# Recurrent branch: one left operand for two products, and its transpose beside them in crossed tiles

## The reference, cut to what matters

```python
def step(S, inp):
    r_t, w_t, k_t, v_t, a_t, b_t = inp
    sa = jnp.einsum('bhij,bhj->bhi', S, a_t)
    S = S * w_t[:, :, None, :] + sa[..., None] * b_t[:, :, None, :] + v_t[..., None] * k_t[:, :, None, :]
    y = jnp.einsum('bhij,bhj->bhi', S, r_t) if emit else None
    return S, y
```

## Time and profile before

| | us |
|---|---|
| median of 3 runs | 2735.48 (2731.41 to 2739.09) |
| profiled execution, its own time | 2739.95 |
| its span in the trace | 2738.2 |
| TensorE busy | 2606.0 |
| VectorE busy | 1708.3 |
| ScalarE busy | 928.2 |
| GpSimd busy | 831.3 |

### The profile page before, as it was taken

How to read it: one execution, slowest core, us unless ns; L and a number is a source line. 1 busy time by engine, 2 the same in 40 slices (tenths; PEclk the granted TensorE clock), 3 DMA queues, 4 the chain that set the end, 5 groups by cost and what they waited for, 6 DMA issues and landing times. The chain is left out here.

```text
span 2738.2 us, 60351 instructions
## 1 busy us (share of the span) xinstructions
PE 2606.0 (95%) x25068; PEld 2077.8 (76%) x25068; DVE 1708.3 (62%) x3073; ACT 928.2 (34%) x2146; POOL 831.3 (30%) x1067
## 2 busy tenths in 40 slices
PE   7989999999999999999999999999999899999998
PEld 4978798795654887868688867777888677858886
DVE  5657767764525846764753358659833676577675
ACT  2013323223422225642221148321211576122571
POOL 3323344240013520012322215235531344246010
PEclk9999999999999999999999999999999999999999
DMA  6321100102432013303011152131111311122100
GB/s 235 106 95 57 45 13 9 39 15 96 156 107 91 32 62 140 125 1 108 33 62 62 62 191 68 53 115 58 36 62 62 139 63 62 62 84 93 79 3 31
DMA packets 108464, 206.05 MB, mean 75 GB/s; under 512 B 21955, under 2 KB 26194, under 8 KB 107680
## 3 DMA queue, kind: packets, MB, share of 16 engines
q1 hardware_dynamic: 107920, 201.30, 21.0%
q0 software_dynamic: 272, 0.89, 0.1%
HBM read 186.85 MB, written 15.54 MB: 74 GB/s over the span
## 5 line engine op out<-in xcount | busy, mean ns | idle before, releaser
L739 PE MATMUL psum<-weights,h_t 128*128 128x256 f32 x1488 | 355.2, 382 | 5.5 <-ACT early_work L828 5.5
L739 PEld LDWEIGHTS psum<-weights,h_t 128*128 128x128 f32 x1488 | 280.8, 191 | 45.3 <-ACT early_work L828 6.7
L739 PE MATMUL psum<-z_l,x_tiles 128*128 128x256 f32 x816 | 192.8, 379 | 0.5 <-POOL z_l L954 0.5
L1528 DVE TENSOR_REDUCE neg_max<-psum 128x1 f32<-128x768 f32 x160 | 147.1, 955 | 69.0 <-PE psum L1304 58.7
L739 PEld LDWEIGHTS psum<-z_l,x_tiles 128*128 128x128 f32 x816 | 155.0, 190 | 21.9 <-issue 0.9
L839 ACT ACTIVATE early_work<-psum 128x512 f32<-128x512 f32 (+1 forms) x80 | 45.0, 565 | 364.7 <-DVE psum L1112 248.1
L1477 ACT ACTIVATE prob<-psum,neg_max 128x768 f32<-128x768 f32 x128 | 114.1, 897 | 80.4 <-DVE neg_max L1528 80.4
L1112 DVE TENSOR_TENSOR psum<-psum,early_work 128x512 f32<-128x512 f32 x62 | 43.1, 696 | 146.3 <-PE psum L739 146.3
L1600 POOL TENSOR_TENSOR z_l<-z_l,inv_total 128x128 f32<-128x128 f32 x64 | 25.3, 400 | 310.4 <-DVE inv_total L1536 310.4
L739 PE MATMUL psum<-weights,x_tiles 128*128 128x256 f32 x496 | 117.2, 379 | 0.0
L790 PE MATMUL psum<-weights,h_t 128*128 128x512 f32 x256 | 111.5, 593 | 1.2 <-PEq L240 1.2
(11 more groups left out here) (545 smaller groups left out, 6661.2 us busy)
## 6 DMA issues: line engine op xcount, KB each, us to landing
weights<-in_ada_w_dram SPq DMA_DIRECT2D x30, 2048.0 KB, 8.2
weights<-in_a_w_in_dram SPq DMA_DIRECT2D x10, 2048.0 KB, 8.0
weights<-in_b_w_in_dram SPq DMA_DIRECT2D x8, 2048.0 KB, 8.6
weights<-in_c_w_in_dram SPq DMA_DIRECT2D x8, 2048.0 KB, 8.8
weights<-in_w_in_dram SPq DMA_DIRECT2D x6, 2048.0 KB, 8.7
x_aside<-x_tiles SPq DMA_DIRECT2D x24, 512.0 KB, 2.6
x_tiles<-x_aside SPq DMA_DIRECT2D x4, 3072.0 KB, 15.9
weights<-in_a_w_out_dram SPq DMA_DIRECT2D x4, 2048.0 KB, 7.9
```

What stands on the lines that cost most here:

```text
L739: last = pe.matmul(dst, lhs[:, k, :], rhs[k // 2][:, k % 2, :], start=k == 0, stop=k == KH - 1)
L1528: dve.tensor_reduce(neg_max[:, i % 4, m:m + 1], score_at(i, m), AX, ALU.max, negate=True)\
```

## The change: what it does

1. **Groups for jobs.** The 20 jobs become six groups: b with the context of both directions, b with the sequence of direction 0, of direction 1, and the same three of k. In a sequence group each chunk and head is one matmul whose left operand is b (or k) and whose streamed side is 128 columns, 64 of a and 64 of r, in two runs of the buffer. In a context group 64 columns of a are streamed.
2. **Crossed tiles.** After the two products of a chunk come its two transposes: that of the head on partitions 0 to 63 is written to PSUM partitions 64 to 127, and the other way round, in banks of their own. ScalarE takes them back across in two copies of 64 partitions each.
3. **Who takes what.** The `nt` product is no longer masked by VectorE. VectorE reads it from PSUM with the mask of level 1 alone, ScalarE copies it out unmasked, and the level masks that follow pick the entries they need. GpSimd adds the identity. VectorE's transposed copies wait for GpSimd.
4. **Banks and waits.** A group's banks are taken again three groups later, after VectorE and ScalarE have read them; the inverse uses banks 0 to 3 in place of 4 to 7. GpSimd's masks of L4043 wait for the first three groups only.

```diff
-            for i, job in enumerate(jobs):
-                name, d, chunks, left, right, _, _ = job
-                if i >= 8:
-                    pe.wait_ge(*done(i - 8))
-                for n, c in enumerate(chunks):
-                    cols = slice(col_of(c), col_of(c) + CH)
-                    for h in range(2):
-                        s = slice(64 * h, 64 * h + 64)
-                        rhs = pr.eye[s, s] if right is None else right[s, d, cols]
-                        last = pe.matmul(pr.bank(i % 8)[s, CH * n:CH * n + CH], left[s, d, cols], rhs,
-                                         start=True, stop=True)
+            def decayed_and_read(s, d, c):
+                at = d * US + col_of(c)
+                step = 2 * US + d * SEQ - d * US
+                return flat_x[s, at:at + 2 * step].rearrange("p (two x) -> p two x", two=2)[:, :, 0:CH]
+            def multiply(g):
...
+                if g >= 3:
+                    for semaphore in seen(g - 3):
+                        pe.wait_ge(*semaphore)
...
+                        for s in halves:
+                            if seg:
+                                last = pe.matmul(pair_ps(g, 0)[s, d, n, :], left[s, d, columns(c)], b["a_f"][s, d, columns(c)],
+                                                 start=True, stop=True)
+                            else:
+                                to = pr.bank(first_bank_of(g), 2)[s, 2 * CH * n:2 * CH * n + 2 * CH]
+                                last = pe.matmul(to.rearrange("p (two t) -> p two t", two=2), left[s, d, columns(c)],
+                                                 decayed_and_read(s, d, c), start=True, stop=True)
+                        for h, s in enumerate(halves):
+                            o = halves[1 - h]
+                            to = turned_ps(g)[o, d, n, :] if seg else turned_ps(g)[o, n, :]
+                            beside = pe.matmul(to, left[s, d, columns(c)], pr.eye[s, s], start=True, stop=True)
                 last.then_inc(*multiplied.tick())
+                beside.then_inc(*turned.tick())
...
@@ block.vector
+            for d in range(2):
+                begin(1, d)
+            for d in range(2):
+                begin(0, d)
+                take("rb", d)
+            mirror_begun(0)
+            mirror_begun(1)
+            take_context()
+            mirror_begun(2)
+            mirror_begun(3)
+            for d in range(2):
+                take("ak", d)
+                take("rk", d)
...
@@ block.scalar
+            def take_n(g):
+                _, seg, d = groups[g]
+                act.wait_ge(*multiplied.at(g + 1))
+                act.wait_ge(*taken_v.at(v_order.index(("nt", seg, 1 if seg else d)) + 1))
...
+            def take_turned(g):
...
+                act.wait_ge(*turned.at(g + 1))
+                for h, s in enumerate(halves):
+                    last = act.activation(out[s], turned_ps(g)[halves[1 - h]], ACT.Copy)
+                last.then_inc(*taken_a.tick())
+            for g in range(3):
+                take_n(g)
+                take_turned(g)
+            for g in range(3, 6):
+                take_turned(g)
...
@@ block.gpsimd
+            for i, (d, seg) in enumerate(batches):
...
+                pool.wait_ge(*taken_v.at(v_order.index(("nt", seg, d)) + 1))
+                pool.tensor_tensor(t, t, wide(single(eye, 1 - d), 1, e - a), ALU.add).then_inc(*added_eye.tick())
+                pool.wait_ge(*taken_a.at(a_order.index(("nt", seg, None if seg else d)) + 1))
...
+                pool.tensor_tensor(b["levels"][0][:, d, a:e, :], b["m_ab_t"][:, d, a:e, :],
+                                   wide(masks[:, MASKS.index(name), :], 1, e - a), ALU.mult).then_inc(*levelled.tick())
```

More of the change, by code:

```diff
@@ L3722, in rwkv_core_stage, with seen, first_bank_of @@
     s_decayed = pr.counter("sc_s_decayed")
[L3723 to L3735, removed]
-    eye = masks[:, MASKS.index("eye"), :]
[L3738 to L3744, removed]
+    groups = [("b", 1, None), ("b", 0, 0), ("b", 0, 1), ("k", 1, None), ("k", 0, 0), ("k", 0, 1)]
+    v_order = [("nt", 1, 0), ("nt", 1, 1), ("nt", 0, 0), ("rb", 0, 0), ("nt", 0, 1), ("rb", 0, 1),
+               ("ak", 1, None), ("ak", 0, 0), ("rk", 0, 0), ("ak", 0, 1), ("rk", 0, 1)]
+    a_order = [("nt", 1, None), ("bt", 1, None), ("nt", 0, 0), ("bt", 0, 0), ("nt", 0, 1), ("bt", 0, 1),
+               ("kt", 1, None), ("kt", 0, 0), ("kt", 0, 1)]
+    eye = masks[:, MASKS.index("eye"), :]
+    flat_x = pr.X[:, :, :].rearrange("p t n -> p (t n)")
+    def seen(g):
+        name, seg, d = groups[g]
+        v = [i for i, x in enumerate(v_order) if x[1] == seg and (d is None or x[2] == d)
+             and x[0] in (("nt", "rb") if name == "b" else ("ak", "rk"))]
+        a = [i for i, x in enumerate(a_order) if x[1] == seg and x[2] == d and x[0] in (("nt", "bt") if name == "b" else ("kt",))]
+        return taken_v.at(max(v) + 1), taken_a.at(max(a) + 1)
+    def first_bank_of(g):
+        return (0, 2, 5, 0, 2, 5)[g]
     def single(x, odd):
@@ L3799, in _ @@
                 last.then_inc(*multiplied.tick())
+                beside.then_inc(*turned.tick())
+            for g in range(len(groups)):
+                multiply(g)
             def products(bank, lhs, rhs, i, half=None):
@@ L3835, in _ @@
                     pe.wait_ge(*x_out.at(i - 1))
-                else:
-                    pe.wait_ge(*done(14 + i))
+                elif i == 0:
+                    for semaphore in seen(3):
+                        pe.wait_ge(*semaphore)
                 products(X + i % 2, n_m[li % 2], b["inv"], i).then_inc(*x_done.tick())
@@ L3933, in _ @@
         def _(dve):
[L3934 to L3952, removed]
-                    dve.transpose(b["inv"][:, d, a:e, :], b["inv_t"][:, d, a:e, :]).then_inc(*begun_mirrored.tick())
@@ new lines, in begin @@
+            def begin(seg, d):
+                a, e = segment(seg)
+                g = 0 if seg else 1 + d
+                src = pair_ps(g, 0)[:, d] if seg else pair_ps(g, 0)
+                cols = dict(two=2)
+                src = src.rearrange("p c (s two) -> p c s two", **cols)[:, :, :, 1 - d]
+                t = b["inv_t"][:, d, a:e, :].rearrange("p c (s two) -> p c s two", **cols)[:, :, :, 1 - d]
+                first = masks[:, MASKS.index(("up1", "low1")[d]), :]
+                dve.wait_ge(*multiplied.at(g + 1))
+                ins = dve.tensor_tensor(t, src, wide(single(first, 1 - d), 1, e - a), ALU.mult)
+                ins.then_inc(*taken_v.tick())
@@ new lines, in mirror_begun, with take @@
+            def mirror_begun(i):
+                d, seg = batches[i]
+                a, e = segment(seg)
+                dve.wait_ge(*added_eye.at(i + 1))
+                dve.wait_ge(*identity.at(d + 1))
+                dve.transpose(b["inv"][:, d, a:e, :], b["inv_t"][:, d, a:e, :]).then_inc(*begun_mirrored.tick())
+            def take(name, d):
+                g = (1 if name == "rb" else 4) + d
+                mask = masks[:, MASKS.index(("up", "low")[d] + ("" if name == "ak" else "_i")), :]
+                dve.wait_ge(*multiplied.at(g + 1))
+                if name == "rb":
+                    dve.wait_ge(*taken_a.at(a_order.index(("nt", 0, d)) + 1))
+                dve.tensor_tensor(b["m_" + name][:, d, 0:XC, :], pair_ps(g, 0 if name == "ak" else 1), wide(mask, 1, XC),
+                                  ALU.mult).then_inc(*taken_v.tick())
```

63 lines of the change are left out of this document (41 added, 22 removed).

## The result

The changed kernel took 2713.9 us (median of 4 runs, 2712.51 to 2718.3) and the kernel before 2733.44 (2730.1 to 2739.09): ratio 0.9933 [0.9919, 0.9947], 19.5 us less. The forecast was 2714.

A forecast was written before the change was run, and what follows sets the result against it. TensorE's record pace was taken as the bound: products 8.9 us for 14.95, `finish(0)` at 11.4 for 16.76, 5.35 less per pair. Over four pairs that is 21.4 us off the median 2735.48, so 2714 us, range 2708 to 2731.

The forecast's parts named there:

- TensorE's pace, four tiles together: Pair products: a chunk's four tiles run together, 0.22 us per sequence chunk, 0.117 per context chunk, 8.9 us for 14.95.
- rival 2: Pair products: only two of four tiles run together, 14.4 us of products, 2730 to 2735 us in all; chance 0.13.
- Rival 1: Pair products: weight loads go in turn on shared partitions, 11.2 us of products, 2721 us in all; chance 0.15.
- Rival 3: Pair products: a tile waits for its neighbour on the same partitions, 25.6 us of products, 2778 us; chance 0.08.
- The sum: Per pair: 8.9 us of products, 9 to 9.5 from first product to inverse, `finish(0)` at 11.4 for 16.76.
- I leave that pair like the rest: Second pair before the change: its products take some 0.9 us more than the first's; treated like the other pairs.
- the wrong-sized term: ScalarE's 15 copies, 0.60 us each, 0.5 start to start, from 1.8 us; `finish(0)` may start at 10.9 or 11.0.
- The forecast of 11.4: `finish(0)` starts 11.4 us after a pair's first product, for 16.76 before: 5.35 us less per pair.
- GpSimd and VectorE's waits: GpSimd's fourth identity addition ends at 9.0 to 9.9 us; VectorE's read that `finish(0)` needs ends at 10.7 to 11.6.
- rival 4: Products shrink, but waits on ScalarE's copy or GpSimd's additions eat the gain; 2725 us with half of it; chance 0.06.
- Worth nothing by itself: VectorE: dropping its two identity instructions (1.38 us each on a sequence block) and the unmasked part of `nt` gains nothing.
- The inverse and the scan follow: Behind the products: inverse and scan keep their instructions and move up whole; the inverse still takes 28.9 us.

The follow-up runs named there:

- e1_diag: Changed kernel with the transposes put back on the diagonal tiles, on their own rows, products still joined: 2732.42 us, ratio 0.9991 to the kernel before.
- e3_same_rows: Changed kernel with a chunk's four matmuls issued head by head, product then transpose: 2721.75 us, ratio 0.9944 to the kernel before.
- e6_repeat: Changed kernel with each pair's first group multiplied nine times over, 512 records more per pair: 2775.99 us, ratio 1.0143 to the kernel before.
- e4_split: Changed kernel, still crossed, with each 128-column product split into two of 64, 512 records per pair: 2730.6 us, ratio 0.9984 to the kernel before.
- e7_no_k_turned: Changed kernel without the transposes of k, 96 records fewer per pair, so another output: 2713.67 us, ratio 0.9925 to the kernel before.
- e8_vector_eye_early: Changed kernel with VectorE adding the identity right behind begin's read, ahead of GpSimd's masks: 2718.37 us, ratio 0.9945 to the kernel before.
- e2_vector_eye: Changed kernel with VectorE, not GpSimd, adding the identity just ahead of each transposed copy: 2739.69 us, ratio 1.0018 to the kernel before.
- e5_early_step: Changed kernel with the inverse's first product issued ahead of the last group: 2718.7 us, ratio 0.9937 to the kernel before.
- run 80: Not a run's label: TensorE "had run 80 records", that is, executed them, in the unaltered changed kernel's rerun (2714.97 us, ratio 0.9925 to the kernel before).

## Why the prediction was right

- **TensorE's pace, four tiles together: held.** A sequence chunk costs 0.22 us, as worked out. Crossing gives this pace (e1_diag without it: 14.47 us), and rival 2, which had just that number, fell. Rival 1, loads in turn, would be 11.2 us; the pairs have 9.4 to 10.5. In the rerun two pairs took 11.6 and 11.8, but of these one has 2.0 us of holes and the other a lower clock.
- **Rival 3 fell** in the changed kernel and again in e3_same_rows, where it would have been 25.6 us of products for 9.31. The rule of the Trainium skill behind it ("TensorE: Matmul & The Clock Gate", "The mechanism": a weight load overlaps a matmul only when its row group is another) does not hold here: the trace has 0.22 us a chunk, where it would have 0.566; two tiles on the same partitions run together in either order.
- **What the pace leaves out: the supply of instructions.** The sum had 8.9 us for the products and "9 to 9.5" to the inverse; two pairs took 10.5. The second had two holes, 10.53 − 9.51 = 1.02 us. The third has no idle time and took 9.43, 0.5 over the sum. Three of its records start late: the first of the fifth and of the sixth group 0.21 and 0.15 us behind the record ahead, 0.14 us after ScalarE has emptied the banks they write (436.27 and 438.11), and record 342 is 0.26 us behind, at the place of a hole. The prediction looked at the time of a record and not at how fast records arrive. That pace is 3.73 us per 128 (e6_repeat); the diagonal tiles of before used 128 x 29.2 ns = 3.74, just at its edge, which fits that no hole stood in the first pair there. The second pair was over it by 0.9 us; the prediction saw these 0.9 us and passed them over ("I leave that pair like the rest"). So I did not see that the supply would become the next bound. It is why both halves of the change are needed: crossing makes records cheap and joining makes them few. Alone they give 0.9984 (e4_split) and 0.9991.
- **ScalarE: the wrong-sized term.** I priced a copy at 0.60 us and 0.5 from start to start, from one pair with a short second copy. It is 0.61: thirteen copies take 234.56 − 226.62 = 7.94 us. The two copies of `n_t` behind them do overlap as priced, 0.60 and 0.38 in 0.87; why the thirteen don't is open. Its start at 1.8 us was right (226.62 − 224.85 = 1.77). So `finish(0)` can't start before 1.8 + 15 x 0.61 + 0.6 = 11.6, not 10.9 to 11.0. Pairs 1 and 3, and the same two of e7_no_k_turned with far fewer records, sit on 11.6 to 11.9. The forecast of 11.4 was a little under this, and with the holes it is 12.7 in two pairs. That makes 19.1 us at `finish(0)` for the forecast 21.4. The scan gained 20.5 all the same, so `finish(0)` was not the right place to measure at: what counted was how much earlier TensorE could begin the inverse.
- **GpSimd and VectorE's waits: held.** In the first pair the fourth addition ended at +9.2 (9.0 to 9.9 forecast). VectorE waited 0.95 us for ScalarE and 0.30 for GpSimd; rival 4 fell.
- **"Worth nothing by itself": held for the kernel as built, and not in general.** With the identity early on VectorE (e8_vector_eye_early) no difference can be told. Behind GpSimd's masks it costs 1.07 and 1.30 us an instruction, a wait of 3 us, then the clock: all of the gain (e2_vector_eye). So the move to GpSimd keeps the addition out of a bad place in VectorE's queue, which I had not looked at.
- **The inverse and the scan follow: held.** 28.9 and 29.75 us in the first and last pair for 28.9 and 29.5 (the earlier trace rows ends its last stretch at 594.60, 0.6 us ahead of the scan); the scan starts 20.5 us earlier in all.
- **The hit to 0.1 us is luck.** The forecast took 21.4 us off a median of 2735.48; with one run more that median is 2733.44, and it fell by 19.5. The profiled execution was 2712.5 for a forecast of 2718.5. Both agree with 20.5 us in the pairs within the spread of the runs, some 6 us.

What stays open: why a packet comes in time at one place and 1 us late at another (0.1 us of idle time or less in pair 3, 1.0 in pairs 2 and 4; the second pair has other transfers at 98 GB/s beside it, the fourth has not), why the granted clock fell in the fourth pair of several runs, and why e5_early_step lost what it should have won. The differences among the changed kernel, e3_same_rows, e5_early_step and e8_vector_eye_early are within their intervals. No version ran that beats the changed kernel. By e7_no_k_turned ScalarE's fifteen copies set `finish(0)`; whether shorter ones would bring the scan forward wasn't tried, and the inverse that absorbed 0.3 us of that wait speaks against much of a gain.

## What to carry to other kernels

Small matmuls on one quarter of the array can run four at a time if the second pair is written crosswise, but then count instructions too: over more than the first packets a pace of records faster than that of their arrival is not to be had (here 29 ns a record), and fusing two matmuls into one of twice the columns is worth more than its streaming time says. When an engine gets relief, price the next one by a long run of its instructions back to back, not by one pair. Put an elementwise operation with two SBUF operands ahead of GpSimd's long ones, or give it away.

## What the runs showed of the hardware that was not expected

- TensorE's instructions came in at one packet of 16 KB, 128 records with their loads, per 3.73 us (e6_repeat). Before, the instruction queue moved 11 packets in the 43.8 us from first product to scan, which is 4.0 us each. Such a mean hides the limit: records 80, 208 and 336 of the second pair started late then too.
- VectorE's addition with both operands in SBUF took 1.07 and 1.30 us beside GpSimd's masks, and 0.46 and 0.29 on average ahead of them. It ended 0.33 or 0.18 us after the mask that was running had given way to the next, so its cost is what is left of that mask. The Trainium skill, page "SBUF — State Buffer", section "Who interferes with whom", has this as a rule: an instruction of VectorE with two SBUF inputs contends with a GpSimd instruction that reads SBUF. The trace agrees, with the sizes above.
- In e2_vector_eye the granted clock fell to its lower level behind a wait of 2.89 us, for most of 12 us, and 32 records took 1.87 us for 1.12. In the changed kernel it stayed at 1.00 behind waits of 0.46 to 0.61. In its rerun it was at the lower level from 528.97 to 535.79, from just ahead of the fourth pair's products; in the 4.7 us before, TensorE had run 80 records with a wait of 1.59 us between them.
- A copy of 64 partitions from PSUM takes ScalarE as long as one of 128 (591 and 597 ns, groups of the changed kernel from 220 to 620), so crossing the halves back costs twice the instructions and twice the time.
